# Sparse attention on one core: the compressed branch of a head is scored, weighed and turned two tiles later

## What is computed

```python
# compressed branch: 31 compressed keys and values of the group
s_c = einsum(qblk, k_cmp) + bias_c
p_c = softmax(where(m_c, s_c, NEG)) * any(m_c)
o_c = einsum(p_c, v_cmp)
# selected branch and window branch: up to 512 keys each
s_s = einsum(qblk, k_g) + bias_s ; p_s = softmax(...) ; o_s = einsum(p_s, v_g)
s_w = einsum(qblk, k_win) + bias_w ; p_w = softmax(...) ; o_w = einsum(p_w, v_win)
o = gate0 * o_c + gate1 * o_s + gate2 * o_w
o = o.reshape(b, s, 1024) * silu(z)
return o @ w_out
```

## Time and profile before

| what | value |
|---|---|
| median of 3 runs | 2213.18 us (2212.07 to 2213.27) |
| the profiled execution | 2209.61 us |
| its span, first to last instruction | 2208.3 us |
| PE busy, share of the span | 2111.7 us, 96% |
| DVE, ACT, POOL busy | 1002.5, 777.8, 255.3 us |
| share of PE on the chain that ended last | 83% (DVE 8%, ACT 5%, issue 4%, POOL 1%) |
| attention stage of the sparse layer | 1625 to 1839 us of the span |
| mean granted TensorE clock | 0.987 |

### The profile page before, as it was taken

The page is one execution under the profiler, slowest core; times in us unless marked ns, Lnnn a source line. Parts: engine busy times, 40 slices in busy tenths (PEclk is TensorE's granted clock), DMA queues, the critical chain, the costliest instruction groups (busy, mean ns, idle before and its releaser), DMA issues.

```text
span 2208.3 us, 26578 instructions
## 1 busy us (share of the span) xinstructions
PE 2111.7 (96%) x10149; PEld 1721.3 (78%) x10149; DVE 1002.5 (45%) x2026; ACT 777.8 (35%) x1485; POOL 255.3 (12%) x360
## 2 busy tenths in 40 slices
PE   6999999999999999999999999999989999899978
PEld 4887887888878875888888888777878888688657
DVE  4437424443354336345434433554355553522575
ACT  4326322222232223332322222333355553332562
POOL 0103000000002110000100000010035552000250
PEclk9999999999999999999999999999999999999999
DMA  4330242333323330332333333253221112333211
GB/s 156 108 96 11 68 124 80 96 99 101 94 97 115 96 96 10 96 96 77 116 99 100 97 96 96 62 158 101 77 73 34 35 35 96 108 96 96 77 39 48
DMA packets 96766, 190.47 MB, mean 86 GB/s; under 512 B 8407, under 2 KB 16639, under 8 KB 96512
## 3 DMA queue, kind: packets, MB, share of 16 engines
q1 hardware_dynamic: 90288, 164.35, 24.2%
q0 software_dynamic: 6352, 24.41, 3.5%
HBM read 184.48 MB, written 4.26 MB: 85 GB/s over the span
## 4 chain that ended last, share of the span: by engine, by line
PE 83%; DVE 8%; ACT 5%; issue 4%; POOL 1%; DMA 0%; ACTq 0%; DVEq 0%; SPq 0%
PE bank L671 64%; PE bank L704 7%; PE bank L1095 3%; PE bank L936 2%; DVE wl L1745 1%; ACT junk L1262 1%; DVE hTl L1817 1%; DVE xn L1807 1%; PE bank L921 1%; PE bank L1006 1%; PE bank L1076 1%; PE bank L1065 1%; PE bank L1102 1%; PE bank L740 1%; DVE pTn L2292 1%
## 5 line engine op out<-in xcount | busy, mean ns | idle before, releaser
L1745 DVE TENSOR_TENSOR wl<-raw,wh 128x1024 fp32r<-128x1024 f32 x306 | 376.8, 1236 | 832.4 <-ACT wh L1223 831.9
L1223 ACT ACTIVATE wh<-raw 128x1024 fp32r<-128x1024 f32 x306 | 320.8, 1053 | 898.1 <-PE bank L671 875.3
L671 PE MATMUL bank<-hTh,wh 128*128 128x512 f32 (+1 forms) x1328 | 517.3, 390 | 0.2 <-issue 0.2
L671 PE MATMUL bank<-hTl,wh 128*128 128x512 f32 (+1 forms) x1328 | 516.7, 389 | 0.0
L671 PE MATMUL bank<-hTh,wl 128*128 128x512 f32 (+1 forms) x1328 | 516.6, 389 | 0.0
L671 PEld LDWEIGHTS bank<-hTh,wh 128*128 128x128 f32 (+1 forms) x1328 | 248.0, 187 | 53.6 <-issue 0.3
L671 PEld LDWEIGHTS bank<-hTh,wl 128*128 128x128 f32 (+1 forms) x1328 | 247.9, 187 | 53.2
L671 PEld LDWEIGHTS bank<-hTl,wh 128*128 128x128 f32 (+1 forms) x1328 | 248.0, 187 | 52.9
L671 PE MATMUL bank<-wh,hTh 128*128 128x512 f32 x464 | 181.6, 391 | 1.3 <-DVE hTl L2445 1.1
L671 PE MATMUL bank<-wh,hTl 128*128 128x512 f32 x464 | 180.6, 389 | 0.0
L671 PE MATMUL bank<-wl,hTh 128*128 128x512 f32 x464 | 180.5, 389 | 0.0
(11 more groups left out here) (351 smaller groups left out, 2773.2 us busy)
## 6 DMA issues: line engine op xcount, KB each, us to landing
raw<-in_ffn_w_in SPq DMA_DIRECT2D x88, 512.0 KB, 3.5
raw<-in_ret_w_in SPq DMA_DIRECT2D x48, 512.0 KB, 3.8
raw<-in_ffn_w_out SPq DMA_DIRECT2D x44, 512.0 KB, 3.7
raw<-in_diff_w_in SPq DMA_DIRECT2D x32, 512.0 KB, 3.7
raw<-in_fox_w_in SPq DMA_DIRECT2D x24, 512.0 KB, 3.8
raw<-in_nsa_w_in SPq DMA_DIRECT2D x20, 512.0 KB, 3.6
raw<-in_ret_w_out SPq DMA_DIRECT2D x16, 512.0 KB, 3.7
bt<-bias_by_lag POOLq DMA_DIRECT2D x16, 448.0 KB, 3.9
```

Source lines behind the costliest of these rows:

```text
L671: i = pe.do.matmul(dst, x, y, start=first and k == 0 and q == 0, stop=stop)
L1223: act.do.activation(M.hl[n % HL_SLOTS][0][:, 0:m], M.raw[n % RAW_SLOTS][:, 0:m], ACT.Copy).then_inc(*T.up("act_hi", n))
L1745: dve.do.tensor_tensor(wl[:, 0:m], M.raw[n % RAW_SLOTS][:, 0:m], wh[:, 0:m].bitcast(F32), ALU.subtract).then_inc(*T.up("dve_lo", n))
```

## The change

All steps of the compressed branch of a head, on all engines, move by two tiles. The scores, the maximum, the subtraction and the exponential went with tile s0 and go with s2; the sum, the reciprocal, the gate, the weighing, the transpose and its copy went with s2 and go with w0. The product with the compressed values stays where it was. Two waits of `cmp_scores` (for the queries) move to `scores(n)`, and DVE's wait for the bias table moves from the compressed step to every `largest(n)`. `pe_by_tile` gets a parameter `mode` that no caller sets.

```diff
     def scores(n):
-        if br == 0 and i == 0:
+        if br == 0 and i == 2:
             pool.wait_ge(*at("dve_cmp", (h, "max")))
...
-        if br == 0 and i == 2:
+        if br == 1 and i == 0:
             pool.wait_ge(*at("dve_gate", "any"))
...
     def cmp_scores(h):
         pe_bank(pe, T, 3)
-        pe.wait_ge(*at("act_q", h // 2))
-        pe.wait_ge(*at("dve_q", h // 2))
...
     def scores(n):
-        if br == 0 and i == 0:
+        if br == 0 and i == 2:
             cmp_scores(h)
         pe_bank(pe, T, b)
+        pe.wait_ge(*at("act_q", h // 2))
+        pe.wait_ge(*at("dve_q", h // 2))
...
     def turn(n):
-        if br == 0 and i == 2:
+        if br == 1 and i == 0:
             pe_bank(pe, T, 3)
             pe.wait_ge(*at("pool_cmp", (h, "weighed")))
...
     def exp(n):
-        if br == 0 and i == 0:
+        if br == 0 and i == 2:
             act.wait_ge(*at("pool_cmp", (h, "less")))
...
     def turned_out(n):
-        if br == 0 and i == 2:
+        if br == 1 and i == 0:
             act.wait_ge(*at("pe_cmp", ("turned", h)))
...
     def largest(n):
-        if br == 0 and i == 0:
+        if br == 0 and i == 2:
             dve.wait_ge(*at("pe_cmp", ("scores", h)))
-            dve.wait_ge(*at(f"bt{h % 2}", h))
...
-        if br == 0 and i == 2:
+        if br == 1 and i == 0:
             dve.wait_ge(*at("act_cmp", h))
...
+        dve.wait_ge(*at(f"bt{h % 2}", h))
         dve.wait_ge(*at("pe_score", ("nsa", n)))
```

More of the change, by code:

```diff
@@ L676, in pe_product, with pe_by_tile @@
         k0 += nk
-def pe_by_tile(pe, T, M, tags, operand, ready, freed, late=None, closes=None):
+def pe_by_tile(pe, T, M, tags, operand, ready, freed, late=None, closes=None, mode="T"):
     banks = [pe.banks4() for _ in tags]
@@ L697, in pe_by_tile @@
                 for k in range(nk):
-                    for name, key in ready(k0 + k, o):
+                    for name, key in ready(k0 + k, o if mode == "T" else None):
                         pe.wait_ge(*T.at(name, key))
                     h, l = operand(k0 + k)
-                    parts = [(h[:, cols], wh[:, k, :]), (h[:, cols], wl[:, k, :]), (l[:, cols], wh[:, k, :])]
+                    if mode == "F":
+                        parts = [(wh[:, k, cols], h), (wh[:, k, cols], l), (wl[:, k, cols], h)]
+                    else:
+                        parts = [(h[:, cols], wh[:, k, :]), (h[:, cols], wl[:, k, :]), (l[:, cols], wh[:, k, :])]
                     for q, (x, y) in enumerate(parts):
```

## The result

| | before | changed |
|---|---|---|
| median | 2212.11 us (22 runs, 2209.16 to 2216.03) | 2216.96 us (22 runs, 2212.75 to 2218.66) |
| ratio | | 1.0019, 95% interval 1.0012 to 1.0025 |
| profiled execution | 2209.61 us | 2218.02 us |

The account below looks back on a forecast made before the run. PE, busy 96% of the span, was taken as the bound. Second and third groups +18.9, first groups -5.3 and -8.7, start -1.4 give +3.5 us on the 2213.2 median: 2216.7 us, range 2211 to 2221.

Parts of the forecast that it names:

- The stall: PE's compressed scores (L1051) wait for ACT's late copy `pcT`, 14 times, 9.1 us; the change was to remove it.
- First groups: Scores of w2 to first products: 4.44 to 3.20 us after even heads, 4.54 to 3.78 after odd.
- Second and third group: Distance to second products, compressed scores now ahead of s2: 4.46 us against 3.20, 1.26 more, 15 times.
- the four steps named: Compressed scores to DVE's bias 1.10, to tile exponential 1.43, to DVE's copy 0.81, to second products 1.12 us.
- rival 1: Compressed branch stays hidden before s2, third group grows only by moved work: -1.1 us, 2212.1; chance 0.10.
- Heads: Per-head terms: +18.9 us for second and third groups, -5.3 and -8.7 for first groups.
- The start: Stretch up to head 0's first products: 0.6 to 1.9 us earlier, taken as -1.4.
- Rival 4: TensorE's clock falls in the stage, about 3.0 us per fall: 2219.7 us; chance 0.07.
- DVE's sum and reciprocal: 0.45 us of DVE ahead of w0's maximum, beside the second products; taken to cost nothing.
- POOL's two steps: Compressed-branch steps on POOL ahead of the weighing of s3 and w0; taken to cost nothing.
- Rival 3: DVE's compressed sum delays w0 and w1, first groups wait longer: 10.6 us on top, 2227.3; chance 0.07.
- Rival 2: Moved scores fill PE's 0.6 us idle per head in the third group: -10.1 us, 2203.1; chance 0.08.

Follow-up runs that it names:

- The longer: Changed kernel with one more POOL multiplication by 1.0 on the compressed rows ahead of the subtraction: 2222.86 us, ratio 1.0046 to the kernel before.
- the shorter round trip: Changed kernel with ACT's compressed exponential issued behind that of s2 instead of ahead of it: 2212.03 us, ratio 0.9997 to the kernel before.

## Why the prediction was right, point by point

- **Total.** Forecast +3.5 us on the median, range 2211 to 2221; measured 2216.96 against the forecast 2216.7, and by the ratio +4.2 us (2.7 to 5.5). That the two absolute numbers are so close is partly luck: the median of before moved from 2213.18 to 2212.11 with more runs.
- **The stall goes and is replaced.** Right: no wait of the compressed scores is left, 7 waits for POOL, 31 for each kind of copy.
- **First groups.** Gains of 1.24 and 0.76 us forecast; measured 1.25 and 0.68. The odd one was too large because PE took up POOL's weight 0.15 us after its end (1744.74 + 0.55 to 1745.44) where I had carried over the 0.06 seen behind DVE's copy. That POOL's low part makes the difference between odd and even heads is shown by the run that moves it: 0.59 of 0.67 us go.
- **Second and third group.** +1.26 forecast, +1.30 measured, in the four steps named. The 0.04 is the first compressed matmul: I took the longer first start for a thing of the wait ahead of it, and it stays also behind products. The longer and the shorter round trip show that the chain is the one named, and rival 1 (hidden) falls; its sign, 4.15 us from the compressed scores to the second products, was not there (4.50).
- **Heads.** 15 x 1.30 - 7 x 0.68 - 7 x 1.25 = +6.0 us; the trace has +6.1, with 0.1 more in the last head (forecast +4.9). The 1.2 us too few are 15 x 0.04, 7 x 0.08 and most of that 0.1.
- **The start.** This term was mis-sized: -1.4 taken, with bounds 0.6 and 1.9; measured -2.0. The three other kernels with the compressed scores at s0 need 11.57, 11.59 and 11.71 us up to the first products, where before took 10.95; the four others with the scores ahead of s2 take 8.87, 8.89, 9.41 and 9.69, where the changed kernel took 8.92. The means are 11.5 and 9.2, so that the move is worth 2.3 us rather than 2.0, more than my upper bound of 1.9. The clock's low stretch differs too. In the changed kernel it was

```profile
1628.90:1635.70 6.80, 5.08 (x17) 3.94 (x18) 4.74 (x25) 5.72 (x18) 3.67 (x8) 0.51 0.25 77
1637.00:1653.00 16.00, 15.23 (x116) 13.13 (x116) 7.39 (x37) 8.32 (x32) 8.14 (x16) 1.00 0.10 33
1653.00:1846.00 193.00, 178.10 (x1328) 153.31 (x1328) 96.52 (x423) 97.69 (x340) 96.05 (x172) 1.00 0.10 32
```

  6.8 us at 1.2 GHz (granted clock 0.51) instead of the 10.1 of the earlier trace rows. The start term thus has an uncertainty of its own of about 0.8 us, which my bounds from DVE's and ACT's steps left out; what part the clock has in it was not taken apart. The errors of the two parts, +1.2 and -0.6 (-0.9 by the means), partly cancel. That the total came out as near as it did is luck to that extent; the larger term, the heads, was 20% too small.
- **The clock in the stage.** Right: full from 1637 on (1.00 in both rows above), in spite of the longer waits. The Trainium skill (TensorE: Matmul & The Clock Gate, "A second HAM failure mode: psum-queue depth-cycling") tells of a bf16 kernel in which frequent short idles between groups of matmuls made the clock swing. This trace does not show it: in 1653 to 1846 PE waited 29 times for ACT's copies and POOL's weights, up to 0.6 us each and 13.0 us in all, at clock 1.00. Rival 4 did not come about.
- **DVE's sum and reciprocal** stayed hidden, as did POOL's two steps: the even first group has exactly its 3.20 us. Rival 3 did not come about.
- **Rival 2** gave its outcome a chance of 0.08 by filling PE's idle time. Its sign, 3.55 us from the compressed scores to the second products, was not there (4.50), and the run with the scores behind s3 shows that this does not work from the second group. The 0.6 us that it wanted to fill are waits of PEld in the earlier trace rows; PE itself, with a matmul still in flight, waited there once, for 0.4 us, in the whole stage. The gain it hoped for is there, but in the transpose's place alone.

## What to carry to other kernels

When an engine waits ahead of some work, look whether the work or what releases it is at the wrong place; here moving both cost 4 us, and moving only the release (a transpose and a copy) gained 10 from first to last products. Before moving a side chain over several engines, find the stretch where its round trip runs beside long work on the bound engine: beside the 2.3 us of the first products it held up nothing, and ahead of the chain that frees bank 5 each hundredth of a microsecond added to it arrived in the total. Price such a move as the distance between two fixed starts, step by step, once for each kind of iteration (the odd heads differed by 0.6 us).

## What the runs showed of the hardware beyond that

The same POOL tile of 128x124 float32 took 0.52 us as a multiplication by a constant (TENSOR_SCALAR) and 0.40 as a subtraction of two tensors, with 0.08 and 0.03 to the next engine's or step's start; I had expected the simpler form to be the quicker one. Programs that are the same up to 1617 us reached that point 4.1 us apart in their profiles, 3.0 of it in two stretches where the clock was at half in one (0.54 and 0.50) and full in the other. Ahead of the first of them the two profiles look alike: in 270 to 277 us PE was busy for 4.65 of 7.00 us in both, at clock 1.00. What decides it the profiles do not show.
